# Moving the second pair's weight split and rotary queries behind the latent queries at the entry of the attention heads

## The chip, the cores and the metric

The kernel runs on one core of a Trainium2 chip. Its engines work side by side and meet through semaphores: TensorE (PE, matmuls into the accumulation banks), VectorE (DVE), ScalarE (ACT), GpSimd (POOL), and SyncE (SP), which here only issues DMAs. Each engine runs its own instructions in the order in which they are written. The metric is the device time in microseconds (us), the median of several runs.

## The reference

Two small networks run one after the other on 512 positions of width 1024. The first has a convolution-like layer and a layer of latent attention with 16 heads; the second has two hybrid layers. The change touches the latent attention alone:

```python
q = jnp.einsum('bsr,rhd->bshd', q_c, w_uq)
q_nope, q_rope = q[..., :MLA_NOPE], q[..., MLA_NOPE:]
q_rope = apply_rope(q_rope, cos[:, :, None, :], sin[:, :, None, :])
q_lat = jnp.einsum('bshd,rhd->bshr', q_nope, w_uk)
...
    s = jnp.einsum('bqhr,bkr->bhqk', ql, kv_c) + jnp.einsum('bqhd,bkd->bhqk', qr, k_rope)
    s = s.astype(jnp.float32) * ATTN_SCALE
    p = jax.nn.softmax(jnp.where(mask, s, -jnp.inf), axis=-1).astype(kv_c.dtype)
    return jnp.einsum('bhqk,bkr->bqhr', p, kv_c)
...
o = jnp.einsum('bshr,rhd->bshd', o_lat, w_uv).reshape(B, S, MLA_WIDTH)
```

So each head has a query from the latent `q_c` (128 columns, `q_nope`, turned into a latent query `q_lat`), a rotary query of 64 columns, scores against all earlier keys in four blocks of 128 queries, a softmax, and a product with the values.

## The kernel before

Everything is float32, but the matmuls take their operands in two parts, a rounded `_hi` and the remainder `_lo`, and add three products (`mm3`: L808 to L810). Making such a pair takes a copy to `_hi` (mostly ACT) and a subtraction to `_lo` (DVE). Weights come in tiles of 128 rows (`w_raw`), and ACT (`split_tile`, L1290) and DVE (L1569) split them as well. In the heads one tile serves a pair of heads; it holds the query, the latent and the value weights of both. The tiles alternate between two buffers.

Each engine walks the same list of steps, and inside a step the order of its instructions is the order of the code. `head_entry` (the rotary queries of the first pair and the first query) stands between two chunks of the layer's gate `sz`. Then come the steps `head` with t = -1, 0, 1 up to 17. At step t PE does the scores of head t (`head_scores`, four blocks i = 0 to 3), the query of head t + 1 (`head_q`, into bank 7), its latent query (`head_ql`, also bank 7), the transposes of the probabilities of head t - 1 (`head_turn`), and its product with the values (`head_pv`; its second half, L1085, waits for all four transposed blocks). A reduction of the conditioning (`redux`, L946, matmuls of one column) stands between the steps -1 and 0.

What the others do in step t:

- DVE: the maximum of each score block (a masking MEMSET and a reduction, `head_max`, L1811 and L1814), the remainders `qn_lo` and `ql_lo` of the query and the latent query of head t + 1, the reciprocals, and the scaling of the probabilities (`p_even` in even heads, `p_odd` in odd ones, L1869). A block's maximum waits for its scores.
- ACT: the exponentials (L1460), the copies `qn_hi` and `ql_hi`, the copies `pT` of the transposed probabilities (L1469; the fourth behind `ql_hi`), the values' copy `v_tok`.
- Once for a pair of heads, the rotary queries of the next pair j: six matmuls on PE (`head_qr`, bank 5); a copy `qr_f` (ACT, L1503); on DVE the product with the cosine into `rope_y` (L1842); on POOL four products with the sine, `rope_t` (L2221); on DVE their sum (`rope_turned`, L1820); two casts `q_rot` on ACT (`cast_rope`, L1488) and two remainders on DVE (`rope_low`, L1826). The first four stand in even steps, the rest in the odd step behind.
- Some steps also split the next pair's weight, and on DVE take one piece of the conditioning's product (`acc`, L1597). `splits_in` says which step splits which tile: the second pair's tile is split in step -1, on ACT ahead of `ql_hi` of the first head, on DVE behind `ql_lo`.

Of the kernel before, what the change touches and what calls it, by code (L numbers as in the profile page):

```python
# [304 lines left out]
def build(nc, wt, adat, colst, matst, rmatst, xt, pos, wst, bst, poolt, decayt, rot, out):  # L305
# [11 lines left out]
    with ExitStack() as ctx:  # L317
# [487 lines left out]
        def _(pe):  # L805
# [283 lines left out]
            for d in steps:  # L1089
# [77 lines left out]
                elif op == "head":  # L1167
# [7 lines left out]
                    if rope_pair_at(t) is not None:  # L1175
                        head_qr(rope_pair_at(t))
# [14 lines left out]
                    if ahead:  # L1191
                        head_ql(t + 1)
                    if before:
# [82 lines left out]
        def _(act):  # L1276
# [94 lines left out]
            for d in steps:  # L1371
# [76 lines left out]
                elif op == "head":  # L1448
# [41 lines left out]
                    if T is not None:  # L1490
                        split_tile(T)
# [7 lines left out]
                    if rope_pair_at(t) is not None:  # L1499
                        j = rope_pair_at(t)  # L1500
                        act.wait_ge(qr_full, j + 1)
                        act.wait_ge(qr_val, j)
                        act.activation(qr_f[:], bank[:, 5, :], ACT.Copy).then_inc(qr_taken, 1)  # L1503
# [8 lines left out]
                    if ahead and t % 2 == 1 and t >= 1:  # L1512
                        cast_rope((t + 1) // 2)
                    if here:
                        exp(2)
                    if ahead:
                        act.wait_ge(ql_full, t + 2)
                        if t >= 0:
                            act.wait_ge(sc_full, NB * (t + 1))
                        act.activation(ql_hi[:], bank[:, 7, :], ACT.Copy).then_inc(ql_hi_done, 1)  # L1520
                    if before:
                        copy_turned(NB - 1)
                    if here:
                        exp(3)
# [37 lines left out]
        def _(dve):  # L1562
# [253 lines left out]

            def rope_turned(j):
# [10 lines left out]
            def head(t):  # L1828
# [11 lines left out]
                if rope_pair_at(t) is not None:  # L1840
                    dve.wait_ge(qr_taken, rope_pair_at(t) + 1)
                    dve.tensor_tensor(rope_y[:], qr_f[:], cos1[:], ALU.mult).then_inc(qr_cos, 1)  # L1842
                if odd:
                    rope_turned(odd)
                if T is not None and t >= 0:
                    split_tile(T)
                if ahead and here:
                    dve.wait_ge(qn_hi_done, t + 2)
                    dve.tensor_tensor(qn_lo[:], bank[:, 7, :], f(qn_hi[:]), ALU.subtract).then_inc(qn_lo_done, 1)
                if here:  # L1850
                    head_max(t, 2)
                    head_max(t, 3)
                if odd:
                    rope_low(odd, 0)
                if ahead:
                    dve.wait_ge(ql_hi_done, t + 2)
                    dve.tensor_tensor(ql_lo[:], bank[:, 7, :], f(ql_hi[:]), ALU.subtract).then_inc(ql_lo_done, 1)
                if odd:
# [12 lines left out]
                if t == -1:  # L1871
                    split_tile(T)
# [468 lines left out]
```

## Time and profile before

| | |
|---|---|
| median of 3 runs | 1378.86 us (1377.54 to 1382.34) |
| the profiled execution | 1380.56 us |
| its span | 1378.8 us |
| PE busy | 1325.2 us, 96% |
| DVE busy | 913.8 us, 66% |
| ACT busy | 563.3 us, 41% |
| POOL busy | 302.2 us, 22% |
| granted clock of PE, mean | 0.99 |

The span runs from the first to the last instruction that the profile shows; the profiled execution's time holds 1.8 us more around it. A timeline has one line for an instruction or for several alike: its start, its duration, the engine, the line of the kernel, what it writes and reads with partitions x elements, how many, and in brackets how long the engine idled before it and what ended that. The entry of the heads lies at about 500 us, the first pair of heads runs to about 533 us, the last head ends at about 665 us.

### The profile page before, as it was taken

The page shows a single profiled execution, that of the slowest core. Times are in us where ns is not written, and L with a number is a line of the kernel's source. Part 1 is how long each engine was busy: PE and PEld are TensorE (multiplying, and loading weights), DVE is VectorE, ACT ScalarE, POOL GpSimd, SP SyncE. Part 2 cuts the span into 40 slices and gives each one's busy share as a digit, 9 for nine tenths or more (in the row PEclk, how much of TensorE's full clock was granted, in tenths as well). Part 3 has the DMA queues.
Part 4 walks back from the last instruction along what each step waited for, and adds up shares of the span by engine and source line. Part 5 has one row for each costly group of instructions (what it writes and reads, how often), then busy time and mean ns, then how long its engine had stood idle before and what let it go on. Part 6 is the DMA issues. An engine that isn't in the chain of part 4 may idle for free. (4 is left out here: it accounts for less than half of the span.)

```text
span 1378.8 us, 17321 instructions
## 1 busy us (share of the span) xinstructions
PE 1325.2 (96%) x6751; PEld 1121.5 (81%) x6751; DVE 913.8 (66%) x1330; ACT 563.3 (41%) x852; POOL 302.2 (22%) x204
## 2 busy tenths in 40 slices
PE   2999999999999999999999999999999999999997
PEld 2998888778888878888888788888878788888875
DVE  6754544774476558988578886685776577675553
ACT  1423322221254246656322475543342466533430
POOL 0200210055420014555344100001115300011123
PEclk9999999999999999999999899999999999999998
DMA  9443333323423321212233242222313322211211
GB/s 372 181 168 138 138 137 137 120 109 138 144 93 138 129 68 68 70 37 91 99 131 138 92 167 108 92 92 92 131 53 140 136 92 74 80 62 61 65 59 61
DMA packets 30609, 155.12 MB, mean 113 GB/s; under 512 B 3392, under 2 KB 3520, under 8 KB 19264
## 3 DMA queue, kind: packets, MB, share of 16 engines
q1 hardware_dynamic: 30528, 154.03, 30.7%
q8 instruction: 53, 0.87, 0.3%
q14 instruction: 28, 0.23, 0.1%
HBM read 151.92 MB, written 2.10 MB: 112 GB/s over the span
## 5 line engine op out<-in xcount | busy, mean ns | idle before, releaser
L808 PE MATMUL bank<-h_lo,w_hi 128*128 128x512 f32 x1008 | 398.1, 395 | 3.6 <-DVE h_lo L1731 1.4
L810 PE MATMUL bank<-h_hi,w_hi 128*128 128x512 f32 x1008 | 393.1, 390 | 0.0
L809 PE MATMUL bank<-h_hi,w_lo 128*128 128x512 f32 x1008 | 392.9, 390 | 0.0
L1569 DVE TENSOR_TENSOR w_lo<-w_raw,w_hi 128x2048 fp32r<-128x2048 f32 (+2 forms) x91 | 206.6, 2270 | 86.0 <-ACT w_hi L1290 85.9
L808 PEld LDWEIGHTS bank<-h_lo,w_hi 128*128 128x128 f32 x1008 | 189.5, 188 | 43.6 <-issue 5.9
L810 PEld LDWEIGHTS bank<-h_hi,w_hi 128*128 128x128 f32 x1008 | 189.3, 188 | 40.0
L809 PEld LDWEIGHTS bank<-h_hi,w_lo 128*128 128x128 f32 x1008 | 189.5, 188 | 37.9 <-issue 0.5
L1290 ACT ACTIVATE w_hi<-w_raw 128x2048 fp32r<-128x2048 f32 (+2 forms) x91 | 166.8, 1833 | 90.0 <-PE bank L810 78.1
L1597 DVE SCALAR_TENSOR_TENSOR acc<-ada_raw,cond,acc 128x1024 f32<-128x1024 f32 x70 | 95.7, 1367 | 0.0
L1366 ACT ACTIVATE tmp<-bank 128x512 f32<-128x512 f32 x48 | 28.6, 595 | 131.2 <-PE bank L810 121.2
L2130 POOL TENSOR_SCALAR q_dup<-rot_y 128x512 fp32r<-128x512 f32 x8 | 11.9, 1492 | 309.6 <-DVE rot_y L1608 309.6
L808 PE MATMUL bank<-mixc_lo,w_hi 128*128 128x512 f32 x128 | 50.8, 397 | 0.0
L810 PE MATMUL bank<-mixc_hi,w_hi 128*128 128x512 f32 x128 | 50.0, 390 | 0.0
L809 PE MATMUL bank<-mixc_hi,w_lo 128*128 128x512 f32 x128 | 49.9, 390 | 0.0
L2047 DVE TENSOR_TENSOR_SCAN keep<-keep 128x127 f32<-128x127 f32 (+2 forms) x64 | 49.0, 807 | 0.4
L946 PE MATMUL bank<-mats,acc 128*128 128x1 f32 x192 | 25.5, 263 | 24.4 <-DVE acc L1597 24.4
L2143 POOL TENSOR_TENSOR sum<-sum,sqr 128x512 f32<-128x512 f32 x24 | 48.0, 2002 | 1.9
L946 PEld LDWEIGHTS bank<-mats,acc 128*128 128x128 f32 x192 | 26.4, 215 | 25.3 <-DVE acc L1597 24.5
L1690 DVE SCALAR_TENSOR_TENSOR x<-bank,gate,x 128x512 f32<-128x512 f32 x16 | 12.0, 751 | 52.3 <-PE bank L810 52.1
L2221 POOL TENSOR_TENSOR rope_t<-qr_f,sin 32x512 f32<-32x512 f32 x28 | 37.9, 1352 | 34.2 <-ACT qr_f L1503 31.8
L808 PE MATMUL bank<-w_lo,h_hi 128*128 128x256 f32 x128 | 37.8, 295 | 4.4 <-DVE h_lo L1731 4.4
L2142 POOL TENSOR_TENSOR sqr<-x 128x512 f32<-128x512 f32 x24 | 36.6, 1525 | 24.7 <-DVE x L1700 23.6
(337 smaller groups left out, 2622.5 us busy)
## 6 DMA issues: line engine op xcount, KB each, us to landing
w_raw<-wt SPq DMA_DIRECT2D x83, 1024.0 KB, 5.8
ada_raw<-adat SPq DMA_DIRECT2D x80, 512.0 KB, 3.7
ada_first<-adat SPq DMA_DIRECT2D x16, 512.0 KB, 10.4
w_raw<-wt SPq DMA_DIRECT2D x8, 640.0 KB, 4.8
spare_raw<-wt SPq DMA_DIRECT2D x3, 1024.0 KB, 5.7
x<-xt SPq DMA_DIRECT2D x4, 512.0 KB, 16.6
out<-outf SPq DMA_DIRECT2D x8, 256.0 KB, 2.2
poolw<-poolt SPq DMA_DIRECT2D x1, 1024.0 KB, 5.6
```

Of the source, the lines that this page charges most:

```text
L808: pe.matmul(dst, ah, bl, start=start, stop=False, skip_group_check=True)
L809: pe.matmul(dst, al, bh, start=False, stop=False, skip_group_check=True)
L810: return pe.matmul(dst, ah, bh, start=False, stop=stop, skip_group_check=True)
L946: ins = pe.matmul(dst[:, j:j + 1], acc[:, u % 2, j * P:(j + 1) * P], ones[:, 0:1], start=True, stop=True)
L1290: act.activation(w_hi[wb[T]][:, 0:n], w_raw[wb[T]][:, 0:n], ACT.Copy).then_inc(w_hi_done, 1)
L1366: act.activation(dst, src, func, scale=scale, bias=bias).then_inc(chunk_taken, 1)
L1569: dve.tensor_tensor(w_lo[wb[T]][:, 0:n], w_raw[wb[T]][:, 0:n], f(w_hi[wb[T]][:, 0:n]), ALU.subtract).then_inc(w_lo_done, 1)
L1597: dve.scalar_tensor_tensor(acc[:, u % 2, :], src, c, acc[:, u % 2, :], ALU.mult, ALU.add).then_inc(ada_done, 1)
L2047: ins = dve.tensor_tensor_scan(k, k, k, 1.0, ALU.mult, ALU.min)
L2142: link(pool.tensor_tensor(sqr[:], x[:, n, :], x[:, n, :], ALU.mult))
L2143: ins = pool.tensor_tensor(sum2[:], sum2[:], sqr[:], ALU.add)
L2221: pool.tensor_tensor(rope_t[to, :], qr_f[of, :], sin1[of, :], ALU.mult).then_inc(qr_turned, 1)
```

## The change

All of it is in the steps t = -1, 0 and 1; from t = 2 on the order is the old one, and no instruction is added or taken away. The second pair's weight split moves from ahead of `ql_hi` of the first head to behind it on ACT, and on DVE from step -1 into step 0, between `qn_lo` and the third maximum. The second pair's rotary queries move on PE from behind the first two score blocks of head 0 to the end of step 0; the copy `qr_f` goes behind `ql_hi` of step 0, the cosine product behind the scaled probabilities of step 0. In step 1 DVE's sum goes behind `ql_lo`, and ACT's two casts from ahead of the third exponential to behind `ql_hi`.

```diff
@@ PE @@
-                    if rope_pair_at(t) is not None:
+                    if rope_pair_at(t) is not None and t > 0:
                         head_qr(rope_pair_at(t))
...
                     if ahead:
                         head_ql(t + 1)
+                    if t == 0:
+                        head_qr(1)
@@ ACT @@
+                    def copy_rope(j):
+                        act.wait_ge(qr_full, j + 1)
+                        act.wait_ge(qr_val, j)
+                        act.activation(qr_f[:], bank[:, 5, :], ACT.Copy).then_inc(qr_taken, 1)
+
-                    if T is not None:
+                    if T is not None and t >= 0:
                         split_tile(T)
...
-                    if rope_pair_at(t) is not None:
-                        j = rope_pair_at(t)
-                        act.wait_ge(qr_full, j + 1)
-                        act.wait_ge(qr_val, j)
-                        act.activation(qr_f[:], bank[:, 5, :], ACT.Copy).then_inc(qr_taken, 1)
+                    if rope_pair_at(t) is not None and t > 0:
+                        copy_rope(rope_pair_at(t))
...
-                    if ahead and t % 2 == 1 and t >= 1:
+                    if ahead and t % 2 == 1 and t >= 3:
                         cast_rope((t + 1) // 2)
...
                         act.activation(ql_hi[:], bank[:, 7, :], ACT.Copy).then_inc(ql_hi_done, 1)
+                    if t == -1:
+                        split_tile(T)
+                    if t == 1:
+                        cast_rope(1)
                     if before:
                         copy_turned(NB - 1)
+                    if t == 0:
+                        copy_rope(1)
                     if here:
                         exp(3)
@@ DVE @@
+            def rope_cos(j):
+                dve.wait_ge(qr_taken, j + 1)
+                dve.tensor_tensor(rope_y[:], qr_f[:], cos1[:], ALU.mult).then_inc(qr_cos, 1)
+
-                if rope_pair_at(t) is not None:
-                    dve.wait_ge(qr_taken, rope_pair_at(t) + 1)
-                    dve.tensor_tensor(rope_y[:], qr_f[:], cos1[:], ALU.mult).then_inc(qr_cos, 1)
-                if odd:
+                if rope_pair_at(t) is not None and t > 0:
+                    rope_cos(rope_pair_at(t))
+                if odd and t > 1:
                     rope_turned(odd)
...
+                if t == 0:
+                    split_tile(splits_in(-1))
                 if here:
                     head_max(t, 2)
                     head_max(t, 3)
-                if odd:
+                if odd and t > 1:
                     rope_low(odd, 0)
                 if ahead:
                     dve.wait_ge(ql_hi_done, t + 2)
                     dve.tensor_tensor(ql_lo[:], bank[:, 7, :], f(ql_hi[:]), ALU.subtract).then_inc(ql_lo_done, 1)
+                if t == 1:
+                    rope_turned(1)
+                    rope_low(1, 0)
                 if odd:
                     rope_low(odd, 1)
...
-                if t == -1:
-                    split_tile(T)
+                if t == 0:
+                    rope_cos(1)
```

The order on ACT at the end of step -1 and in step 0, in the kernel before:

```order
L1366 ACTIVATE sz<-bank 128x512 [waits chunk_full]
L1290 ACTIVATE w_hi_85<-w_raw_83 128x1280 [waits chunk_full,w_landed0]
L1520 ACTIVATE ql_hi<-bank 128x512 [waits ql_full]
L1366 ACTIVATE red<-bank 128x8 [waits post_done,chunk_full]
L1460 ACT_TABLE_LOAD
L1460 ACTIVATE p_even_127,esum<-bank,neg_max 128x128 [waits max_done]
L1503 ACTIVATE qr_f<-bank 128x512 [waits qr_val,qr_full]
L1460 ACTIVATE p_even_128,esum<-bank,neg_max 128x256 [waits max_done]
L1509 ACTIVATE qn_hi<-bank 128x512 [waits ql_full,qn_full]
L1460 ACTIVATE p_even_129,esum<-bank,neg_max 128x384 [waits max_done]
L1520 ACTIVATE ql_hi<-bank 128x512 [waits sc_full,ql_full]
L1460 ACTIVATE p_even_130,esum<-bank,neg_max 128x512 [waits max_done]
```

The same place in the changed kernel:

```order
L1368 ACTIVATE sz<-bank 128x512 [waits chunk_full]
L1524 ACTIVATE ql_hi<-bank 128x512 [waits ql_full]
L1292 ACTIVATE w_hi_85<-w_raw_83 128x1280 [waits chunk_full,w_landed0]
L1368 ACTIVATE red<-bank 128x8 [waits post_done,chunk_full]
L1462 ACT_TABLE_LOAD
L1462 ACTIVATE p_even_127,esum<-bank,neg_max 128x128 [waits max_done]
L1462 ACTIVATE p_even_128,esum<-bank,neg_max 128x256 [waits max_done]
L1513 ACTIVATE qn_hi<-bank 128x512 [waits ql_full,qn_full]
L1462 ACTIVATE p_even_129,esum<-bank,neg_max 128x384 [waits max_done]
L1524 ACTIVATE ql_hi<-bank 128x512 [waits sc_full,ql_full]
L1495 ACTIVATE qr_f<-bank 128x512 [waits qr_val,qr_full]
L1462 ACTIVATE p_even_130,esum<-bank,neg_max 128x512 [waits max_done]
```

The first `ql_hi` changed places with the split, and `qr_f` went from behind the first exponential to ahead of the fourth.

The order on ACT in step 1, from the copy of the values' second half on, in the kernel before:

```order
L1478 ACTIVATE v_tok_140<-bank 128x512 [waits v_full]
L1488 ACTIVATE q_rot_137<-rope_y 64x512 [waits qr_val]
L1488 ACTIVATE q_rot_138<-rope_y 64x512
L1460 ACTIVATE p_odd_133,esum<-bank,neg_max 128x384 [waits rsum_done,max_done]
L1520 ACTIVATE ql_hi<-bank 128x512 [waits sc_full,ql_full]
L1469 ACTIVATE pT<-bank 128x4x128 [waits t_full]
L1460 ACTIVATE p_odd_134,esum<-bank,neg_max 128x512 [waits rsum_done,max_done]
```

The same place in the changed kernel:

```order
L1480 ACTIVATE v_tok_140<-bank 128x512 [waits v_full]
L1462 ACTIVATE p_odd_133,esum<-bank,neg_max 128x384 [waits rsum_done,max_done]
L1524 ACTIVATE ql_hi<-bank 128x512 [waits sc_full,ql_full]
L1490 ACTIVATE q_rot_137<-rope_y 64x512 [waits qr_val]
L1490 ACTIVATE q_rot_138<-rope_y 64x512
L1471 ACTIVATE pT<-bank 128x4x128 [waits t_full]
L1462 ACTIVATE p_odd_134,esum<-bank,neg_max 128x512 [waits rsum_done,max_done]
```

The two casts now stand between `ql_hi` and the fourth `pT`; the semaphore `qr_val` that they wait for is raised by DVE's sum.

The order on DVE from the scaled probabilities of step 0 to the second remainder of the rotary queries in step 1, in the changed kernel, in two pieces. The first is the end of step 0:

```order
L1887 TENSOR_SCALAR p_even_130<-p_even_130,rsum 128x512 [waits rsum_done]
L1829 TENSOR_TENSOR rope_y<-qr_f,cos_121 128x512 [waits qr_taken]
L1607 SCALAR_TENSOR_TENSOR acc<-ada_raw,cond,acc 128x1024 [waits ada_done,ada_landed0]
L1821 MEMSET bank 64x64 [waits sc_full]
L1824 TENSOR_REDUCE neg_max<-bank 128x1 [waits exp_done,dve_in_order]
```

The cosine product is new between the probabilities and `acc`. The second is the end of step 1:

```order
L1824 TENSOR_REDUCE neg_max<-bank 128x1 [waits exp_done,dve_in_order]
L1872 TENSOR_TENSOR ql_lo<-bank,ql_hi 128x512 [waits ql_hi_done]
L1834 TENSOR_TENSOR rope_y<-rope_y,rope_t 128x512 [waits qr_turned,qr_cos]
L1840 TENSOR_TENSOR q_rot_137<-rope_y,q_rot_137 64x512 [waits qr_hi_done]
L1840 TENSOR_TENSOR q_rot_138<-rope_y,q_rot_138 64x512 [waits qr_hi_done]
L1884 RECIPROCAL rsum<-esum 128x1 [waits p_done,exp_done] x4
```

The sum came from between the second maximum and the weight split of step 1, and the first of the two `q_rot` from ahead of `ql_lo`.

## Rows read from the trace of the kernel before

**Rows 1.** The page's first part: busy time, share, instructions of each engine.

```profile
PE 1325.2 (96%) x6751; PEld 1121.5 (81%) x6751; DVE 913.8 (66%) x1330; ACT 563.3 (41%) x852; POOL 302.2 (22%) x204
```

**Rows 2.** Windows: length, busy us of each engine (count), granted clock, DMA share.

```profile
480.00:500.00 20.00, 20.00 (x90) 16.58 (x89) 9.76 (x12) 5.87 (x9) 0.00 (x0) 1.00 0.35 119
...
504.10:507.70 3.60, 3.60 (x10) 2.81 (x10) 1.31 (x7) 1.26 (x4) 0.12 (x1) 0.53 0.00 0
...
520.00:560.00 40.00, 39.58 (x246) 34.37 (x245) 35.25 (x87) 24.76 (x69) 22.56 (x16) 1.00 0.17 56
```

**Rows 3.** Timeline of PE, from the reduction to the second head's scores.

```profile
500.03 1.84 PE L946 MATMUL bank<-mats,acc 128*128 128x1 f32 x16
502.75 0.30 PE L808 MATMUL bank<-kv_lo,ql_hi 128*128 128x128 f32 x1 [0.88 <-ACT red L1366]
...
504.10 0.63 PE L808 MATMUL bank<-qc_lo,w_hi 128*128 128x512 f32 x1
...
512.86 0.33 PE L808 MATMUL bank<-kv_lo,ql_hi 128*128 128x128 f32 x1 [1.41 <-DVE ql_lo L1857]
```

**Rows 4.** Timeline of ACT, the same stretch.

```profile
500.17 1.27 ACT L1290 ACTIVATE w_hi<-w_raw 128x1280 fp32r<-128x1280 f32 x1
501.35 0.58 ACT L1520 ACTIVATE ql_hi<-bank 128x512 fp32r<-128x512 f32 x1
...
510.80 0.58 ACT L1460 ACTIVATE p_even<-bank,neg_max 128x384 f32<-128x384 f32 x1 [1.46 <-DVE neg_max L1814]
...
511.49 0.60 ACT L1520 ACTIVATE ql_hi<-bank 128x512 fp32r<-128x512 f32 x1
511.98 0.68 ACT L1460 ACTIVATE p_even<-bank,neg_max 128x512 f32<-128x512 f32 x1
```

**Rows 5.** Timeline of DVE, the same stretch.

```profile
502.57 1.48 DVE L1569 TENSOR_TENSOR w_lo<-w_raw,w_hi 128x1280 fp32r<-128x1280 f32 x1
...
509.37 0.69 DVE L1849 TENSOR_TENSOR qn_lo<-bank,qn_hi 128x512 fp32r<-128x512 f32 x1 [1.15 <-ACT qn_hi L1509]
...
512.97 1.53 DVE L1869 TENSOR_SCALAR p_even<-p_even,rsum 128x128 f32<-128x128 f32 x4
514.42 1.27 DVE L1597 SCALAR_TENSOR_TENSOR acc<-ada_raw,cond,acc 128x1024 f32<-128x1024 f32 x1
```

**Rows 6.** Timelines of DVE and POOL: cosine and sine products of the second pair.

```profile
507.53 0.69 DVE L1842 TENSOR_TENSOR rope_y<-qr_f,cos 128x512 f32<-128x512 f32 x1 [2.18 <-ACT qr_f L1503]
...
507.58 5.86 POOL L2221 TENSOR_TENSOR rope_t<-qr_f,sin 32x512 f32<-32x512 f32 x4 [31.80 <-ACT qr_f L1503]
```

**Rows 7.** Timeline of DVE in step 1: the first two maxima.

```profile
515.71 0.11 DVE L1811 MEMSET bank<- 64x64 f32 x1
...
516.29 0.42 DVE L1814 TENSOR_REDUCE neg_max<-bank 128x1 f32<-128x256 f32 x1
```

**Rows 8.** Timeline of ACT in step 1.

```profile
517.56 0.60 ACT L1509 ACTIVATE qn_hi<-bank 128x512 fp32r<-128x512 f32 x1
...
518.51 1.28 ACT L1488 ACTIVATE q_rot<-rope_y 64x512 fp32r<-64x512 f32 x2
...
521.02 0.59 ACT L1469 ACTIVATE pT<-bank 128x512 f32<-128x512 f32 x1
```

**Rows 9.** Timeline of PE: the second half of the first value product.

```profile
522.07 1.06 PE L1085 MATMUL bank<-pT,v_tok 128*128 128x128 f32 x8
```

**Rows 10.** Groups by form, DVE, 500 to 660 us: busy us, mean ns.

```profile
L1869 DVE TENSOR_SCALAR p_even<-p_even,rsum 128x256 f32<-128x256 f32 x8 | 9.0, 1126 | 0.0
...
L1869 DVE TENSOR_SCALAR p_odd<-p_odd,rsum 128x256 f32<-128x256 f32 x7 | 2.4, 347 | 0.0
```

**Rows 11.** Timelines of DVE and POOL in a later even head.

```profile
532.89 1.39 DVE L1869 TENSOR_SCALAR p_even<-p_even,rsum 128x256 f32<-128x256 f32 x1
...
531.50 2.62 POOL L2221 TENSOR_TENSOR rope_t<-qr_f,sin 32x512 f32<-32x512 f32 x2
```

## The prediction

> **What bounds the kernel now.** I read the page first: TensorE (PE) is busy 96% of the span [rows 1], so only what lets PE start sooner, or makes it wait, moves the end. The change touches about 25 us, the entry of the attention heads. I read that stretch by windows, then the timeline of each engine. In the heads proper, 520 to 560 us, PE is busy 39.58 of 40 us [rows 2], so whatever the entry gains or loses arrives at the end almost in full. The entry has three losses. After the reduction's one-column matmuls (500.03 + 1.84 = 501.87) PE waits 0.88 us for the first scores; before the second head's scores it waits 1.41 us [rows 3]. The first wait is put down to ACT `red`, but the scores need no `red`: they need `ql_lo`, whose source `ql_hi` stands on ACT behind the 1.27 us split of the second pair's weight [rows 4]. And from 504.10 to 507.70 the granted clock is 0.53 [rows 2], mostly the lower level, 1.2 of 2.4 GHz: some nine matmuls of 512 columns in 3.6 us, 0.4 us each, against 90 in 20 us, 0.22 each, at the full clock from 480 to 500 [rows 2].
>
> **The split behind the first latent query.** On ACT `ql_hi` no longer waits for the split: it can start where the split started, 500.2 instead of 501.35 [rows 4], 1.15 us sooner, and so `ql_lo` is ready at 501.5. PE leaves the reduction at 501.87, so the scores start at 501.9, **0.85 us sooner**, and are over at about 503.3 instead of 504.1, where the matmuls behind them start [rows 3]. No DMA is issued differently, and SP's queue stands as before.
>
> **The first head, followed to the second head's scores.** The two maxima take 515.71 to 516.29 + 0.42 = 1.00 us on DVE [rows 7]; from there to the start of `qn_hi` ACT needs 0.85 us for two exponentials (to 517.56) [rows 8]; the copy takes 0.60. So 503.3 + 1.0 + 0.85 + 0.6 = 505.8, and `qn_lo` (0.69 [rows 5]) ends at 506.5. PE has finished the second query before that, even at the low clock. Now DVE meets its moved split: 1.48 us [rows 5], about 0.1 of it overlapped, to 507.85. What stands behind it is the third and fourth maximum, and ACT's third exponential waits for them. From the start of `qn_lo` (509.37) to that exponential (510.80) it was 1.43 us [rows 4, 5], 0.74 without `qn_lo`: so it starts at 508.6, `ql_hi` 0.69 later (510.80 to 511.49) at 509.3, and the second head's scores 1.37 later (511.49 to 512.86 [rows 3, 4]) at 510.65. That is **2.2 us sooner** than 512.86. The rotary query's six matmuls now start at 508.0, when the split is done, and fit in front of these scores.
>
> **The rotary work meets the probabilities.** This is the step on which the sign turns. Before, POOL's four turned products ran from 507.58 for 5.86 us [rows 6], while DVE had little for them to disturb. Now `qr_f` is copied behind `ql_hi`, 0.49 us after its start (509.8), done at 510.4; POOL runs from there to about 516. ACT's last exponential starts at 510.3, and DVE's `p_even` 0.99 us after it (511.98 to 512.97 [rows 4, 5]), at 511.25: in the middle of POOL's work. What the two do to each other is in the heads behind: a 128x256 `p_even` takes 1.126 us on average, a `p_odd` of the same form, in the heads where POOL has no turned products, 0.347 [rows 10]. One instance shows how: it starts at 532.89, while POOL's product ends at 531.50 + 2.62 = 534.12, and ends itself at 534.28 [rows 11], 1.04 us over its undisturbed time. The `p_even` in front of it had gone through, POOL's next product came, and this one waited: they take turns. The Trainium skill ("SBUF — State Buffer", Who interferes with whom) says that the shared port pair goes for a whole instruction to whichever of the two starts first; it settles that there is a wait, not who starts first in each turn here.
>
> On DVE stand `p_even` x4 (512.97 to 514.42, 1.45), then the moved cosine product (0.69 [rows 6]) and the conditioning piece `acc` (514.42 to 515.71, 1.29 [rows 5, 7]). Undisturbed they end at 511.25 + 1.45 + 0.69 + 1.29 = 514.7, 1.0 sooner than 515.71. With turns: the first waits until POOL's first product ends (510.4 + 1.3 = 511.7, each 1.31 by 2.62 for two [rows 11]), 0.5; three more products get in between, 3 x 1.04 = 3.1. So the second head's first maximum starts between 514.7 and 518.3. I take **518.3**, since each of the four products has a DVE operation beside it that needs the same port; that is 2.6 us later than before.
>
> **The rotary cast in front of the last turned copy.** On ACT the two casts of `q_rot` moved behind `ql_hi` of the third query, and so stand ahead of the copy of the fourth turned block, `pT`, for which the second half of the first head's value product waits on PE. The casts wait for DVE's sum, which now stands behind `ql_lo`. The chain from the memset: 1.00 to the end of the maximum, 0.85 to `qn_hi`, 0.63 to `qn_lo` (DVE's split of this step lies beside this), 1.43 to the exponential, 0.69 to `ql_hi`, 0.63 to `ql_lo`, 0.69 for it, 0.69 for the sum (taken as the cosine product [rows 6]), 0.03, the casts 1.28, 0.03, `pT` 0.59 [rows 8], 0.04: 8.6 us. From 518.3 that is 526.9. Before, PE came to that product at 522.07 with no wait [rows 9], and `pT` (521.02 + 0.59) was ready. So PE is **4.8 us late** there. The 2.2 won earlier is in this already; it becomes waiting: some 2 to 3 us for `qn_lo` and some 3 us for `pT`. I give back 0.2 for the small waits in the next head: **+4.6**. Behind it every step keeps its distance to PE, since the heads' work is as it was.
>
> **The clock.** Before, the level fell after 2.7 us of one-column matmuls and waiting, and the nine low matmuls cost about 9 x 0.2 = 1.8 us [rows 2, 3]. That drop may stay or go; it costs nothing now, because its stretch ends in a wait. But two new waits of some 3 us, with 2.4 us of work between them, are as idle as what preceded it. Another drop behind 526.9 would fall on matmuls of 512 columns and cost between 0 and 1.8. I take the middle, 0.9. The Trainium skill ("TensorE: Matmul & The Clock Gate", What's actually happening) calls the low level the default that activity lifts; taken strictly, it favours the upper end, 1.8, and a sum of 6.4.
>
> **The sum** is 4.6 + 0.9 = +5.5 us. The profiled execution took 1380.56 us for a span of 1378.8; with the change it would be 1386.1. It stands 1.7 over the median of 1378.86, which I use as the base: 1384.4.
>
> **Rivals.** *The port costs nothing, only the casts hold the copy:* the maximum starts at 514.7, PE goes on at 514.7 + 8.6 = 523.3, 1.2 late: 1380.1. If DVE keeps the port once it has it (each of its operations starts before the last one ends), it waits 0.5 once: 1380.6. Rows 11 speak against both, though only for a pair of operations. Anything between this and +4.1 counts as no change. *The gain is kept,* ending on the other side of the base: the casts come early enough that `pT` is ready when PE arrives, at 522.07 - 2.2 = 519.9; then the 2.2 us stand, 1376.7, and with the old clock drop gone as well (1.8) 1374.9. It decides when the memset starts by 519.9 - 8.6 = 511.3; by the order of instructions I find no way there. *Worse:* the waits make the clock fall twice on the path, or the late fourth exponential holds the next head's probabilities as well: +8 to +10, about 1388.
>
> **How the numbers follow.** About 0.3% (4.1 us) is what a measurement of this kernel can tell from no change. Forecast, port turns and held copy, +4.1 to +6.4: 0.70. Port cost small or partial, +1 to +4.1: 0.17. Gain kept: 0.05. Worse: 0.08. Of the forecast case a tenth to a fifth may measure under the bound, since its lower end lies on it: slower 0.64, no change 0.34, faster 0.02. The range leaves out the kept gain and the lower third of the partial case, and the upper half of the worse one: 1380.4 to 1387.2.
>
> **What would show it.** Right: first scores about 0.85 us and second head's scores about 2.2 us sooner; `p_even` of the first head some 4 to 5 us long in all instead of 1.5; a PE wait of 2 to 3 us for `qn_lo` and one of about 3 us ahead of L1085 for `pT`, released through the casts; PE busy in 520 to 560 down by some 4 us. Wrong: `p_even` at 1.5 us with POOL beside it (port), no wait at L1085 (casts), or a wait in the heads behind that was not there before.

## The result, and the profile after

The changed kernel took 1386.2 us (median of 4 runs, 1385.31 to 1388.09), the kernel before 1379.11 (4 runs, 1377.54 to 1382.34): ratio 1.0048, 95% interval 1.0034 to 1.0063. A second series (e8) gave 1.0037 (1.0023 to 1.0051). So it is slower: the medians differ by 7.1 us in the first series and by 5.6 in the second. The profiled execution took 1385.38 us, its span is 1383.6, 4.8 more than before.

Its page and three windows of its trace (length, busy us of PE, PEld, DVE, ACT, POOL with counts, granted clock, DMA share, GB/s):

```profile
PE 1326.2 (96%) x6751; PEld 1121.2 (81%) x6751; DVE 916.4 (66%) x1330; ACT 563.6 (41%) x852; POOL 302.6 (22%) x204
```

```profile
521.90:525.60 3.70, 3.23 (x11) 2.15 (x9) 2.59 (x5) 2.30 (x6) 0.00 (x0) 0.54 0.10 40
504.10:507.70 3.60, 3.50 (x16) 2.49 (x14) 2.13 (x3) 1.41 (x5) 0.00 (x0) 1.00 0.00 0
520.00:560.00 40.00, 37.59 (x222) 32.00 (x223) 33.12 (x84) 23.84 (x62) 19.97 (x14) 0.96 0.15 54
```

PE does 1.0 us more and the span is 4.8 longer: the rest is waiting. From 520 to 560 PE is busy 2.0 us less than in [rows 2]. The low level of the clock that stood from 504.1 to 507.7 in [rows 2] is not there; one stands from 521.9 to 525.6.

PE's timeline (start, duration, line, operation, count, and in brackets the idle time before and what ended it), to be held against [rows 3, 9]:

```profile
500.23 1.84 PE L946 MATMUL bank<-mats,acc 128*128 128x1 f32 x16
501.93 0.31 PE L808 MATMUL bank<-kv_lo,ql_hi 128*128 128x128 f32 x1
...
510.67 0.33 PE L808 MATMUL bank<-kv_lo,ql_hi 128*128 128x128 f32 x1 [0.97 <-DVE ql_lo L1872]
...
521.01 0.50 PE L808 MATMUL bank<-qn_lo,w_hi 128*128 128x512 f32 x1 [2.82 <-DVE qn_lo L1862]
...
522.36 2.77 PE L1081 MATMUL bank<-pT,v_tok 128*128 128x384 f32 x6
526.16 1.16 PE L1085 MATMUL bank<-pT,v_tok 128*128 128x128 f32 x8 [1.03 <-ACT pT L1471]
```

DVE and POOL, against [rows 5 to 7], and ACT, against [rows 4, 8]:

```profile
511.16 3.71 DVE L1887 TENSOR_SCALAR p_even<-p_even,rsum 128x128 f32<-128x128 f32 x4
514.79 1.78 DVE L1829 TENSOR_TENSOR rope_y<-qr_f,cos 128x512 f32<-128x512 f32 x1
516.50 1.27 DVE L1607 SCALAR_TENSOR_TENSOR acc<-ada_raw,cond,acc 128x1024 f32<-128x1024 f32 x1
517.78 0.11 DVE L1821 MEMSET bank<- 64x64 f32 x1
```

```profile
510.46 5.57 POOL L2239 TENSOR_TENSOR rope_t<-qr_f,sin 32x512 f32<-32x512 f32 x4 [34.48 <-ACT qr_f L1495]
```

```profile
524.21 1.28 ACT L1490 ACTIVATE q_rot<-rope_y 64x512 fp32r<-64x512 f32 x2 [1.36 <-DVE rope_y L1834]
525.51 0.60 ACT L1471 ACTIVATE pT<-bank 128x512 f32<-128x512 f32 x1
```

The entry is won as told (501.93, 510.67), and then lost twice: `p_even` takes 3.71 us beside POOL's 5.57, and the fourth `pT` stands behind the casts, which wait 1.36 us for the sum.

**One clock for all traces.** Up to the reduction the executions differ by up to 2.3 us (it starts between 498.30 and 500.57). From here on every time is given with the start of the reduction's matmuls (L946) set to 500.03, its place in the trace of before. Four places follow: the second head's first scores; the second head's first MEMSET on DVE; P1, the second half of the first head's value product (L1085); P3, the same product of the third head. From P3 to the last head the distance of any two traces changes by less than 0.2 us.

| kernel | ratio to before (95%) | scores | MEMSET | P1 | P3 | low clock |
|---|---|---|---|---|---|---|
| before | | 512.86 | 515.71 | 522.07 | 542.75 | 504 to 508 |
| e12 before, again | 1.0004 (0.9992 to 1.0015) | 511.28 | 514.59 | 520.52 | 541.50 | none |
| changed | 1.0048 (1.0034 to 1.0063) | 510.47 | 517.58 | 525.96 | 546.63 | 522 to 526, ahead of P1 |
| e8 changed, again | 1.0037 (1.0023 to 1.0051) | 510.48 | 517.57 | 525.95 | 548.14 | 526 to 530, behind P1 |
| e1 split alone | 0.9991 (0.9981 to 1.0001) | 511.97 | 515.27 | 521.21 | 542.20 | 503 to 507 |
| e11 split alone, again | 0.9988 (0.9979 to 0.9997) | 510.91 | 514.21 | 520.15 | 541.14 | none |
| e2 rotary alone | 1.0033 (1.0019 to 1.0047) | 511.22 | 519.18 | 527.55 | 551.16 | 503 to 507, 524 to 534 |
| e3 casts back | 1.0024 (1.0014 to 1.0034) | 510.87 | 518.18 | 524.11 | 545.08 | 503 to 507 |
| e4 POOL narrow | 1.0019 (1.0010 to 1.0029) | 511.39 | 514.94 | 523.33 | 546.97 | 503 to 507, 523 to 530 |
| e5 both | 0.9987 (0.9975 to 0.9999) | 510.47 | 514.02 | 519.96 | 540.93 | none |
| e6 casts behind | 1.0034 (1.0022 to 1.0046) | 510.47 | 517.57 | 525.00 | 545.91 | 522 to 525, ahead of P1 |
| e9 POOL late | 1.0025 (1.0014 to 1.0036) | 511.29 | 516.99 | 522.92 | 543.90 | none |
| e7 query first | 1.0003 (0.9993 to 1.0013) | 510.03 | 513.67 | 520.28 | 542.16 | none |
| e10 query first, acc kept | 0.9995 (0.9986 to 1.0004) | 510.03 | 514.88 | 520.82 | 541.81 | none |

Two things can be read from the table alone. From the MEMSET to P1 it is 5.93 or 5.94 us wherever the casts stand ahead of the third exponential (e1, e3, e5, e9 to e12; in before 6.36 and in e7 6.61, where PE itself was not there sooner), and 8.37 to 8.39 where they are moved (changed, e8, e2, e4). And the MEMSET tells what the probabilities and the cosine product lose beside POOL: it stands at 517.58 in the changed kernel and at 514.02 in e5, where POOL's products are narrow and the order up to there is the same.

### The profile page after: what moved, and what is told of

It reads as the page before. It is cut to its first block and busy times, and to the rows that moved or that the text cites. A ratio compares the mean times of both kernels' runs of the same rounds, so it can differ in the third digit from the quotient of the medians.

```text
span 1383.6 us, 17321 instructions
## 1 busy us (share of the span) xinstructions
PE 1326.2 (96%) x6751; PEld 1121.2 (81%) x6751; DVE 916.4 (66%) x1330; ACT 563.6 (41%) x852; POOL 302.6 (22%) x204
## 5 line engine op out<-in xcount | busy, mean ns | idle before, releaser
L946 PE MATMUL bank<-mats,acc 128*128 128x1 f32 x192 | 25.5, 263 | 24.7 <-DVE acc L1607 24.7
L946 PEld LDWEIGHTS bank<-mats,acc 128*128 128x128 f32 x192 | 26.4, 215 | 25.5 <-DVE acc L1607 24.7
```

What stands on the lines that cost most here:

```text
L946: ins = pe.matmul(dst[:, j:j + 1], acc[:, u % 2, j * P:(j + 1) * P], ones[:, 0:1], start=True, stop=True)
```

## The experiments

**e1 and e11: the split alone.** To the kernel before:

```diff
-                    if T is not None:
+                    if T is not None and t >= 0:
                         split_tile(T)
...
                         act.activation(ql_hi[:], bank[:, 7, :], ACT.Copy).then_inc(ql_hi_done, 1)
+                    if t == -1:
+                        split_tile(T)
```

> The kernel before, with one part of the change: on ScalarE the second pair's weight split stands behind the first ql_hi. VectorE's split and all rotary work stay where they were. Theory (the split is the good part, the rotary move is the bad one): the first scores start at about 501.9 us instead of 502.75, the rotary query of pair 1 waits at most 0.2 us for w_lo, and if the low clock stretch of 504.1 to 507.7 goes with the wait of 0.88 us, qn_lo comes at about 507.0 instead of 509.37 and the second head's scores at about 510.5 instead of 512.86. The end is 0.8 us (the clock falls as before) to 2.4 us (it does not) sooner than before: ratio 0.9983 to 0.9994. Rival (the gain is eaten on the way, because p_even now starts while POOL's turned products run): the head behind starts no sooner, ratio 1.000. Rival (the moved split is what costs): slower than before, ratio above 1.001.

> The split part alone once more (as e1_split_only), with more runs. In e1 the first value product's second half came 0.86 us sooner than before and the next head's 0.54 sooner, with the low level of the clock from 503 to 507 in both. Theory: the same again, ratio 0.999 to 0.9998; if this execution has no low level there, both come up to 1.8 us sooner than in e1, since PE is behind its weight there and not waiting. Rival: no gain that a measurement tells from nothing, ratio 0.9998 to 1.0005.

e1 took 1379.6 us against 1380.3, e11 1378.19 against 1380.52. P1 came 0.86 us sooner than in the trace of before with the low level in both, and 0.37 sooner than in e12 with the low level in neither. The split is the good part: by the medians 0.7 and 2.3 us. Of the versions with all their work it is the only one with an interval under 1, and only in e11; e1's reaches 1.0001. That it beats the kernel before by anything like 2.3 us isn't shown, since the traces give 0.4 to 0.9.

**e2: the rotary part alone.** The changed kernel with

```diff
-                    if T is not None and t >= 0:
+                    if T is not None:
                         split_tile(T)
...
-                    if t == -1:
-                        split_tile(T)
...
-                if t == 0:
-                    split_tile(splits_in(-1))
...
+                if t == -1:
+                    split_tile(T)
```

> The changed kernel, with both splits of the second pair's weight back at their old place: the rotary part of the change alone. Theory: the loss is all in this part. The wait of 0.88 us ahead of the first scores is back, the second head's scores still start at about 510.7 us (the rotary query is out of their way, and no split stands between qn_lo and the third maximum), p_even of the first head again lies under POOL's products and takes some 3.7 us instead of 1.45, the casts again hold the fourth turned copy, and the third head's scores start some 4 us later than before (522.88): ratio 1.003 to 1.005. Rival (the split in VectorE's row between qn_lo and the third maximum makes the loss): the third head's scores at most 1 us later than before, ratio 1.000 to 1.001.

1385.15 us against 1380.3. Its timelines of DVE and PE:

```profile
512.14 3.69 DVE L1883 TENSOR_SCALAR p_even<-p_even,rsum 128x128 f32<-128x128 f32 x4
```

```profile
521.95 0.50 PE L808 MATMUL bank<-qn_lo,w_hi 128*128 128x512 f32 x1 [2.80 <-DVE qn_lo L1860]
...
527.10 2.07 PE L1085 MATMUL bank<-pT,v_tok 128*128 128x128 f32 x8 [1.43 <-ACT pT L1471]
```

The loss is in the rotary part: 4.85 us by the medians, with neither split moved. The rival by which VectorE's split ahead of the third maximum makes it falls. The trace, the slowest execution of its six, shows more: the scores come at 511.22, not at the 510.7 expected, `qr_f` then waits 0.77 us for its query, and the MEMSET is 1.60 later than in the changed kernel. Its two stretches at the low level have a part in that.

**e3: sum and casts at their old places.** The changed kernel with

```diff
-                    if ahead and t % 2 == 1 and t >= 3:
+                    if ahead and t % 2 == 1 and t >= 1:
                         cast_rope((t + 1) // 2)
...
-                    if t == 1:
-                        cast_rope(1)
...
-                if odd and t > 1:
+                if odd:
                     rope_turned(odd)
...
-                if odd and t > 1:
+                if odd:
                     rope_low(odd, 0)
...
-                if t == 1:
-                    rope_turned(1)
-                    rope_low(1, 0)
```

> The changed kernel, with the rotary sum, the casts and the first low part of pair 1 back at the places that they have in all other odd heads (the sum behind two maxima, the casts ahead of the third exponential). Theory (the held copy is worth some 2 us of the loss): the fourth turned block is copied as soon as ql_hi is done, the wait at L1085 for pT goes, VectorE's chain gets 0.65 us longer by the sum, and the third head's scores start at about 525.4 us instead of 527.08: 1.7 us sooner than the changed kernel, ratio to before about 1.002 to 1.0035. The p_even row keeps its 3.7 us and the second head's first memset stays at 517.8. Rival (only the port costs, the copy's wait hides the low clock and nothing else): within 0.5 us of the changed kernel, ratio 1.0043 to 1.0055.

1383.59 us against 1380.3. `pT` is no longer waited for:

```profile
524.15 1.06 PE L1085 MATMUL bank<-pT,v_tok 128*128 128x128 f32 x8
```

P1 is 1.85 us sooner than in the changed kernel, and the MEMSET 0.60 later, because the low level stood at the entry this time. From MEMSET to P1 it is 5.93 instead of 8.38: the held copy costs **2.45 us**.

**e4: POOL's products over 8 columns.** The changed kernel with

```diff
-                            pool.tensor_tensor(rope_t[to, :], qr_f[of, :], sin1[of, :], ALU.mult).then_inc(qr_turned, 1)
+                            w = 8 if j == 1 else S
+                            pool.tensor_tensor(rope_t[to, 0:w], qr_f[of, 0:w], sin1[of, 0:w], ALU.mult).then_inc(qr_turned, 1)
```

> The changed kernel, with POOL's four turned products of pair 1 over 8 columns instead of 512, all semaphores kept. This leaves most of that pair's turned part of the rotary query out. Theory (VectorE and POOL take turns at a shared port): p_even of the first head takes 1.45 us instead of 3.71, the cosine product 0.7 instead of 1.78, and the second head's first memset comes at about 514.7 us instead of 517.8. From there the chain of 8.4 us to the second half of the value product is as it was, so that product starts at about 523.1 instead of 526.2 and the third head's scores at 524.0 instead of 527.1: 3.1 us sooner than the changed kernel, ratio 1.001 to 1.0025. Rival (p_even is slow for another reason, or POOL is not what delays the second head): memset still at 517 or later, ratio 1.004 to 1.0055.

1382.92 us against 1380.3. DVE and PE:

```profile
512.42 1.26 DVE L1887 TENSOR_SCALAR p_even<-p_even,rsum 128x128 f32<-128x128 f32 x4
```

```profile
523.87 2.08 PE L1085 MATMUL bank<-pT,v_tok 128*128 128x128 f32 x8 [2.46 <-ACT pT L1471]
```

The MEMSET comes at 514.94, where 514.7 was expected, P1 at 523.33 (523.1). But the low level falls behind P1 and the third head's product is no sooner than in the changed kernel: the granted clock in this trace,

```profile
524.00:526.00 2.00, 2.00 (x10) 2.00 (x11) 1.63 (x9) 0.93 (x3) 0.00 (x0) 0.50 0.00 0
526.00:528.00 2.00, 2.00 (x11) 2.00 (x11) 0.93 (x2) 0.00 (x0) 0.91 (x1) 0.50 0.00 0
528.00:530.00 2.00, 2.00 (x6) 1.53 (x6) 0.94 (x4) 0.00 (x0) 1.87 (x2) 0.50 0.00 0
```

Its profiled execution (1385.16 us) was the slowest of its ten, as was e2's (1388.28) of its six, so the others probably lost less to the clock than these traces show. e4 and e5 leave out most of that pair's turned part: they price the meeting with POOL and are no kernels to use.

**e5: both.** e3's and e4's edits together.

> The casts and the sum at their old places (as in e3_casts_back) and POOL's four turned products of pair 1 over 8 columns (as in e4_pool_narrow; most of that pair's turned part is left out). All times with the start of the reduction's matmuls set to 500.03 us as in the kernel before. Theory (the port and the held copy are the whole loss): the second head's first memset comes at about 515.0, as in e4, and the chain from there to the second half of the value product takes 5.9 us, as in e3, instead of 8.4. So that product starts at 520.9 instead of 522.07, with no wait for pT: 1.2 us sooner than before, and the gain of the entry is kept. Ratio 0.9985 to 0.9997. Rival (something else in the change costs as well, such as VectorE's split ahead of the third maximum): the product at 522 or later, ratio 1.000 or above.

1378.85 us against 1380.24.

```profile
511.26 1.25 DVE L1882 TENSOR_SCALAR p_even<-p_even,rsum 128x128 f32<-128x128 f32 x4
...
514.32 0.11 DVE L1819 MEMSET bank<- 64x64 f32 x1
```

```profile
520.26 1.06 PE L1085 MATMUL bank<-pT,v_tok 128*128 128x128 f32 x8
```

Without the two causes the gain of the entry stays: P1 at 519.96, 6.0 us sooner than in the changed kernel, of which 3.56 stand in the MEMSET (517.58 to 514.02, the port) and 2.44 behind it (the copy). Both traces have the full clock at the entry. The two causes add, and nothing is left over: P1 is even 0.56 us sooner than in e12.

**e6: the casts behind the copy, on ACT alone.** The changed kernel with `copy_turned(NB - 1)` ahead of `cast_rope(1)`.

> The changed kernel with one exchange on ScalarE: the casts of pair 1 stand behind the copy of the fourth turned block, not ahead of it. Times with the reduction's start at 500.03. Theory (only the copy was held by them, but q_rot itself is as late): pT is copied at about 522.8, the wait at L1085 for pT is gone or under 0.5 us, and the third head's scores then wait for q_rot, whose last low part ends at about 526.1, so they start at about 526.1 instead of 526.9: 0.8 us sooner than the changed kernel, ratio 1.003 to 1.0045. Rival (the order of the two on ScalarE is the whole of what e3 gained): the third head's scores at 525.2 or sooner, ratio 1.0015 to 1.003.

1385.12 us against 1380.24, not to be told from the changed kernel. PE:

```profile
522.96 2.63 PE L1081 MATMUL bank<-pT,v_tok 128*128 128x384 f32 x6
525.42 1.06 PE L1085 MATMUL bank<-pT,v_tok 128*128 128x128 f32 x8
526.24 0.31 PE L808 MATMUL bank<-kv_lo,ql_hi 128*128 128x128 f32 x1
```

The wait for `pT` is gone and P1 is 0.96 us sooner, as expected, but not for my reason: the scores did not wait for `q_rot` (its first remainder was done at 525.78 of this trace, 0.46 ahead of them). PE was late by itself, since the first half ran at the low level, 2.63 us instead of 1.46. What the exchange is worth at the full clock stays open.

**e9: the port alone, in the kernel before.** One wait more on POOL, nothing left out:

```diff
                         pool.wait_ge(qr_val, j)
+                        if j == 1:
+                            pool.wait_ge(exp_done, 3)
                         for i in range(4):
```

> The kernel before, with one wait more: POOL starts pair 1's four turned products only when the first head's third exponential is done (about 511.4 us, instead of 507.58), so that they lie beside p_even. Nothing else is moved and nothing left out. Times with the reduction's start at 500.03. Theory (VectorE and POOL take turns at the port): p_even takes some 3.7 us instead of 1.53, acc behind it up to 1.0 us more than 1.27, so the second head's first memset comes at 517.9 to 518.9 instead of 515.71; the chain from there to the second half of the value product takes 5.9 us as in e3 and e5, so it starts at 523.8 to 524.8 instead of 522.07: 1.8 to 2.8 us later, ratio 1.001 to 1.0025. Rival (p_even was slow in the changed kernel for what stands around it there, not for POOL): p_even 1.5 us, ratio 1.000 (0.9993 to 1.0007).

1383.6 us against 1380.52. DVE and POOL:

```profile
511.90 4.39 DVE L1869 TENSOR_SCALAR p_even<-p_even,rsum 128x128 f32<-128x128 f32 x4
516.21 1.27 DVE L1597 SCALAR_TENSOR_TENSOR acc<-ada_raw,cond,acc 128x1024 f32<-128x1024 f32 x1
```

```profile
510.58 5.43 POOL L2223 TENSOR_TENSOR rope_t<-qr_f,sin 32x512 f32<-32x512 f32 x4 [34.29 <-ACT p_even L1460]
```

`p_even` is 2.40 us longer than in e12 (1.99), whose clock is full as well, and MEMSET, P1 and P3 are 2.40 later. This shows the price of meeting POOL's products without any other part of the change. Against the first trace, from which the expectation was made, P1 is only 0.85 us later, where 1.8 to 2.8 was expected: that trace had the low level and this one has not. `acc`, for which up to 1.0 us more was expected, began when POOL was through and kept its 1.27. The kernel before pays a little of this too: POOL's products end at 513.44 there, beside the last of `p_even` (1.53 us from 512.97), and in e12, where `p_even` starts 1.58 sooner, it takes 1.99 instead of the free 1.25. Work that reads a bank loses nothing: the maximum of 512 columns takes 0.69 us beside POOL in before and the same without it in the changed kernel:

```profile
510.98 0.69 DVE L1814 TENSOR_REDUCE neg_max<-bank 128x1 f32<-128x512 f32 x1
```

```profile
508.85 0.69 DVE L1824 TENSOR_REDUCE neg_max<-bank 128x1 f32<-128x512 f32 x1
```

The Trainium skill ("SBUF — State Buffer", Who interferes with whom) says that the shared pair of ports is held for a whole instruction; four scalings that take 1.25 us when POOL's products are narrow (e5) and 3.7 to 4.4 beside the full ones agree with that. The runs show these times; that a port is what the two engines share they don't show by themselves.

**e7 and e10: the query first.** e1, with the rotary query of pair 1 on PE behind the second head's query, `qr_f` copied behind `qn_hi`, the cosine product behind `ql_lo`; in e7 `acc` moved as well, to the end of the second head's step.

> A version meant to beat both: the split part alone (e1_split_only), and TensorE makes the second head's query ahead of the rotary query of pair 1; qr_f is copied behind qn_hi, the cosine product stands behind ql_lo, and the conditioning piece acc of the first head's step is moved to the end of the second head's step. Theory (times with the reduction at 500.03): the second head's scores start at about 510.3 instead of 512.86; p_even takes 3 to 3.7 us beside POOL, but acc's 1.27 us no longer stand behind it, so the second head's first memset comes at about 514.4 and the second half of the first value product at 520.3 instead of 522.07: 1.8 us sooner than before, ratio 0.9980 to 0.9992. Rival (p_even and the cosine product beside POOL, and acc in the busy second step, eat it): no sooner than e1_split_only, ratio 0.9990 to 1.001.

> As e7_query_first, but the conditioning piece acc stays at the end of the first head's step, as in the kernel before. Times with the reduction's start at 500.03. Theory (e7 lost in the second head's step, by acc ahead of sz and the maxima, 1.2 of its 1.8 us): the second head's first memset comes 1.27 us later than in e7, at about 514.9, the second half of the value product at about 520.9 (chain 5.9), 1.2 us sooner than before, and the wait of 1.03 us for qn_lo at the third head is gone, so that 0.9 to 1.2 us stay: ratio 0.9988 to 0.9995. Rival (what an execution loses to the low level of the clock decides, not the order): within 0.0005 of 1.000.

e7 took 1380.43 us against 1380.24, e10 1379.66 against 1380.52. In e7 P1 comes at 520.28 as expected, and the next head takes it back, so that the ratio falls into the rival's range:

```profile
527.96 0.51 PE L808 MATMUL bank<-qn_lo,w_hi 128*128 128x512 f32 x1 [1.03 <-DVE qn_lo L1860]
```

In e10 this wait is gone, but P3 is 0.31 us later than in e12. Its ratio of 0.9995 fits the theory and the rival alike, so e10 decides nothing between them. Neither measured under e11: 1.25 us at the scores (511.28 to 510.03) end as nothing, since the MEMSET hardly moves (514.59 to 514.88, the cosine product now lies ahead of `p_even`).

**e8 and e12: the two kernels again.**

> The changed kernel once more, for a second trace and a tighter ratio. The rows of the instruction order (first memset of the second head 17.5 us behind the reduction's start, second half of the value product 25.9 us behind it) should repeat to 0.3 us. The granted clock need not: in e3 and e4, whose code is the same up to there, the low level stood from 503.6 to 507.6 us, and in the first trace of the changed kernel it did not. Theory (the low level behind the reduction is a matter of the single execution, and hidden): if it stands this time, the value product moves by under 0.7 us, since PE waits for qn_lo and pT. If the low level falls behind the second half of the value product instead of ahead of it, as in e2 and e4, the following head is 3.1 us later. Ratio 1.0035 to 1.005.

> The kernel before, unchanged, for a second trace of it. Times with the reduction's start at 500.03. In its first trace the granted clock was low from 504.1 to 507.7 us; in e9, whose code is the same up to the third exponential, it was not, and the second head's scores started at 511.29 instead of 512.86. Theory (part of what separates the two kernels' medians, 5.6 to 5.9 us, from the 3.9 us that their first traces show at the value product is this low level): in a trace of this kernel without it, the second head's scores start at about 511.3, the second half of the first value product at about 520.5 instead of 522.07, and the next head's at 530.6 instead of 532.12; in a trace with it all three stand where they stood. Rival (the product is held by something else): it stands at 521.5 or later although the clock is full. Ratio 0.999 to 1.001 either way.

e8 took 1385.8 us against 1380.24, e12 1379.86 against 1378.97. e8's PE, and two windows of it:

```profile
524.22 1.94 PE L1085 MATMUL bank<-pT,v_tok 128*128 128x128 f32 x8 [2.46 <-ACT pT L1471]
```

```profile
524.00:526.00 2.00, 1.78 (x9) 1.78 (x10) 1.61 (x9) 1.25 (x4) 0.00 (x0) 0.60 0.00 0
526.00:528.00 2.00, 2.00 (x12) 2.00 (x12) 1.28 (x3) 0.00 (x0) 0.56 (x1) 0.55 0.00 0
```

P1 repeats to 0.01 us, and P3 is 1.51 us later, by the clock alone; 3.1 was expected for a low level behind P1, after e2 and e4, where it lasted longer. e12's window, and its PE:

```profile
504.10:507.70 3.60, 3.60 (x19) 3.09 (x18) 1.81 (x5) 2.07 (x6) 2.28 (x2) 1.00 0.00 0
```

```profile
510.15 0.33 PE L808 MATMUL bank<-kv_lo,ql_hi 128*128 128x128 f32 x1 [1.41 <-DVE ql_lo L1857]
...
519.39 1.06 PE L1085 MATMUL bank<-pT,v_tok 128*128 128x128 f32 x8
```

At the full clock the kernel before has its scores at 511.28 (511.3 expected), P1 at 520.52 (520.5) and P3 1.25 us sooner. So the first trace of before was one of its less lucky executions at this place, and the comparison of the two first traces, 3.9 us at P1, understates the change: against e12 it is 5.44 at P1, 5.1 to 6.6 at P3, 6.8 to 6.9 in the span (1383.6 and 1383.7 against 1376.8). The spans hold the work ahead of the reduction as well: it ended 1.3 us later than e12's in the first trace and 0.6 sooner in e8.

## Why the prediction was right

The forecast was 1384.4 us, 5.5 over its base; the medians of two series say 7.1 and 5.6, and the cause is the one forecast. The 7.1 is inside the range but above the +4.1 to +6.4 of the forecast case. Its steps:

- *First scores 0.85 us sooner, second head's scores 2.2.* 501.93 against 502.75, and 510.67 against 512.86 [rows 3]. Right. But most of the second is the clock's: against e12 it is 0.81.
- *Port turns, MEMSET at 518.3.* `p_even` 3.71 us instead of 1.53 [rows 5], the cosine product 1.78 instead of 0.69 [rows 6]; MEMSET at 517.78 in its own trace. Right in kind, 0.5 too late: the four scalings and the cosine product lost 2.46 and 1.10, 3.56 us in all, where 0.5 + 3 x 1.04 = 3.6 was told; but the scalings go at 1.25 us undisturbed (e5), where I took the 1.45 of [rows 5]. That DVE had little for POOL to disturb before was not quite so: in e12 `p_even` takes 1.99.
- *Held copy, chain of 8.6 us.* 8.38, and 5.94 without it. Right; PE's wait ahead of L1085 is 2.46 in e8 and e4, and 1.03 in the first trace, where 1.3 us of it went into the low clock. The 2.82 for `qn_lo` was told as 2 to 3.
- *P1 4.8 us late.* 4.09 by the first pair of traces (3.89 on one clock), 5.44 against e12. The 0.2 given back behind it: 0.3 by e12 (P3 5.13).
- *The old low level: nothing on the path of the changed kernel, 1.8 us at most in before.* Mis-sized in before: 1.55 us at P1 and 1.25 at P3, by e12. And not quite hidden in the changed one: with the low level at the entry the MEMSET came 0.60 us later in e3 (against the changed kernel) and 0.92 in e4 (against e5).
- *A new low level, 0 to 1.8 us, 0.9 taken.* It came in both traces of the changed kernel: 0 in the first, where it fell ahead of P1 and ended in a wait, 1.6 in e8. The upper bound was too low: from P1 to the next head's product it is 10.1 us in the first trace, 11.7 in e8, and 13.1 and 13.2 in e2 and e4, so up to 3.1.
- *"Behind it every step keeps its distance to PE."* True through the heads, not beyond: between 703 and 924 us the changed kernel won back 1.09 us on before, and between 1069 and 1100 it lost 1.90, both by the granted clock (740 to 780: 0.96 against 0.87; 1060 to 1100: 0.91 against 1.00). This was in no term. It nets +0.8 of the span's 4.8. The second pair of traces repeats it: at the same places e8 wins back 0.7 on e12 and loses 1.4, with 0.96 against 0.91 and 0.91 against 0.96. So it may belong to the order rather than to chance; no run decides that. The windows of before, then those of the changed kernel:

```profile
740.00:780.00 40.00, 38.43 (x185) 32.14 (x185) 31.94 (x48) 13.88 (x15) 10.77 (x9) 0.87 0.37 139
1060.00:1100.00 40.00, 38.84 (x189) 31.94 (x189) 26.59 (x34) 15.97 (x22) 15.31 (x12) 1.00 0.32 119
```

```profile
740.00:780.00 40.00, 37.54 (x192) 31.41 (x190) 30.27 (x44) 12.14 (x13) 10.34 (x7) 0.96 0.44 158
1060.00:1100.00 40.00, 40.00 (x182) 33.59 (x181) 24.85 (x31) 12.96 (x14) 16.59 (x12) 0.91 0.34 124
```

Of the signs that were to show it, three were sized too high: `p_even` 3.71 us instead of 4 to 5, the wait for `pT` 2.46 at most instead of 3, and PE busy from 520 to 560 down by 2.0 instead of 4, since 1.8 us of the wait for `qn_lo` lie ahead of 520. And the range does not follow from the words beside it: +1.5, its lower end, leaves out a sixth of the partial case and not a third, and without the upper half of the worse one it would end at +9, not at +8.3.

That the sum of 5.5 lies so near is partly luck: against the trace it was made on, P1 is 0.7 less late than told, and what the clock does (1.25 in that trace's entry, 0 or 1.5 behind P1, 0.8 far behind) makes up for it. How often an execution has each of these low levels, and so how the 5.6 and 7.1 us of the medians divide between order and clock, these traces don't tell.

## What to carry to other kernels

An engine that runs beside another at no cost is only as free as what the other does in that stretch: before moving a copy that starts GpSimd's work, look for VectorE's work between SBUF tiles at the new time, not at the old one. A step that is moved ahead of a copy on an in-order engine is priced by the latest thing that it waits for, here a sum moved behind `ql_lo`, and not by its own 1.28 us. Where a clock drop stands in a trace, take a second trace of the same kernel before counting it, since it may be that execution's.

## What the hardware did that I had not expected

- The same code ran the same stretch at either level. In before, from 504.1 to 507.7, the granted clock was 0.53, in e12 1.00; in both PE had done 1.84 us of one-column matmuls and waited 0.88. In the changed kernel's code up to there (the first trace, e3 to e6, e8) it fell twice in six. The Trainium skill ("TensorE: Matmul & The Clock Gate", What's actually happening) says of a kernel's start that the same kernel meets the low level differently from run to run; e12 and e8 show it in the middle of one.
- A drop is not bounded by what it cost at another place. After a wait of 2.80 us and 1.5 us of work the low level of e2 lasted from 523.5 to 533.7 us of its trace, with a wait of 1.43 us inside it and PE busy throughout from 527.10 on. In e4 it stood in every window from 524 to 530 of its trace, behind a wait of 2.46 us, although PE was busy throughout from 523.87 on.
